# Prompt retention moved beside the gate projection; decode retention in column tiles; decode attention by itself

## What is computed

```python
# retention over the prompt, in 8 chunks of 128 tokens, 4 heads, key 256, value 512
def ret_chunk(S, q, k, v, log_gamma):
    qk = einsum('bihd,bjhd->bhij', q, k) * decay           # 128 x 128
    o = einsum('bhij,bjhe->bihe', qk, v)                   # inner part
    o = o + einsum('bihd,bhde->bihe', q * q_dec, S)        # part across chunks
    S_new = exp(C*log_gamma) * S + einsum('bjhd,bjhe->bhde', k * k_dec, v)
    return S_new, o
# the same function, once, for 8 samples of 8 tokens, each with its own state S (256 x 512 for each head)
# differential attention of 8 heads x 2 maps: the samples' new queries meet 512 cached keys and values
#   that lie in 4 pages of 128 rows, found through page_table
# merge: r = rms_plain(o) * silu(gr);  m = sigmoid(gate_a+b_a)*(a @ w_pa) + sigmoid(gate_b+b_b)*(r @ w_pb)
# h = h + m @ w_o;  h = h + swiglu(rms_norm(h));  y = rms_norm(h)
```

## Time and profile before

| | |
|---|---|
| runs, us | 3125.0, 3123.01, 3119.56 (median 3123.01) |
| profiled execution, us | 3118.55 |
| its span, first to last instruction, us | 3116.8 |
| PE, DVE, ACT, POOL busy | 95%, 33%, 20%, 30% |
| mean granted TensorE clock | 0.98 of full |
| the chain that ended last | PE 80%, issue 12%, DVE 4%, DMA 2% |
| gates beside decode retention, 965 to 1510 us | PE busy 540.05 of 545 us |
| between the stages, 1510 to 1526 us | PE busy 2.80 of 16 us |
| mixers, 1526 to 1868 us | PE busy 313.85 of 342 us |

### The profile page before, as it was taken

The page is one execution under the profiler, slowest core; times in us unless marked ns, Lnnn a source line. Parts: engine busy times, 40 slices in busy tenths (PEclk is TensorE's granted clock), DMA queues, the critical chain, the costliest instruction groups (busy, mean ns, idle before and its releaser), DMA issues.

```text
span 3116.8 us, 40394 instructions
## 1 busy us (share of the span) xinstructions
PE 2960.8 (95%) x15330; PEld 2439.5 (78%) x15330; DVE 1043.3 (33%) x1853; ACT 619.9 (20%) x1339; POOL 924.4 (30%) x782
## 2 busy tenths in 40 slices
PE   6999999999989999999797997999989999999998
PEld 4788887776766778777554557999779999998886
DVE  5430476566663121110133332242341111112323
ACT  3111111554542011111232331110120000001111
POOL 5334354022012223322200000443523343342521
PEclk9999999999999999999898998999989999999999
DMA  4332322332322433343566643443311221214311
GB/s 154 112 103 74 116 75 103 115 114 84 119 77 80 147 136 130 117 137 115 188 217 208 194 154 131 147 141 111 104 50 50 74 75 56 75 62 126 98 57 58
DMA packets 241445, 349.47 MB, mean 112 GB/s; under 512 B 26418, under 2 KB 138418, under 8 KB 241202
## 3 DMA queue, kind: packets, MB, share of 16 engines
q1 hardware_dynamic: 241330, 347.94, 33.5%
HBM read 249.91 MB, written 106.89 MB: 114 GB/s over the span
## 4 chain that ended last, share of the span: by engine, by line
PE 80%; issue 12%; DVE 4%; DMA 2%; POOL 1%; ACT 1%; SPq 0%; POOLq 0%; DVEq 0%; ACTq 0%
PE psum L438 38%; PE psum L414 25%; PE psum L940 5%; PE psum L979 2%; PE psum L1840 2%; PE psum L1003 2%; PE psum L1829 2%; PE psum L993 1%; POOL w_l L277 1%; PE psum L964 1%; POOL w_h L272 1%; DMA edge<-a_t 0%; PE psum L983 0%; DVE xt_l L2159 0%; DVE acc L2268 0%
## 5 line engine op out<-in xcount | busy, mean ns | idle before, releaser
L272 POOL TENSOR_TENSOR w_h<-stage,ones 128x512 fp32r<-128x512 f32 x372 | 416.9, 1151 | 1793.7 <-PE psum L438 950.9
L438 PE MATMUL psum<-xt_h,w_h 128*128 128x384 f32 (+1 forms) x2400 | 542.1, 334 | 23.7 <-DVE xt_l L2159 21.6
L438 PE MATMUL psum<-xt_h,w_l 128*128 128x384 f32 (+1 forms) x2400 | 529.5, 329 | 0.0
L438 PE MATMUL psum<-xt_l,w_h 128*128 128x384 f32 (+1 forms) x2400 | 529.1, 329 | 0.0
L277 POOL TENSOR_TENSOR w_l<-stage,w_h 128x512 fp32r<-128x512 f32 x372 | 491.6, 1352 | 7.4
L438 PEld LDWEIGHTS psum<-xt_h,w_h 128*128 128x128 f32 x2400 | 404.8, 189 | 101.2 <-issue 76.7
L414 PE MATMUL psum<-w_h,xt_h 128*128 128x512 f32 x1120 | 445.4, 398 | 17.0 <-ACTq L608 7.0
L414 PE MATMUL psum<-w_h,xt_l 128*128 128x512 f32 x1120 | 443.9, 396 | 0.0
L414 PE MATMUL psum<-w_l,xt_h 128*128 128x512 f32 x1120 | 443.7, 396 | 0.0
L438 PEld LDWEIGHTS psum<-xt_h,w_l 128*128 128x128 f32 x2400 | 408.5, 189 | 0.0
L438 PEld LDWEIGHTS psum<-xt_l,w_h 128*128 128x128 f32 x2400 | 408.0, 189 | 0.0
(11 more groups left out here) (212 smaller groups left out, 3227.5 us busy)
## 6 DMA issues: line engine op xcount, KB each, us to landing
stage<-in_w_in_dram SPq DMA_DIRECT2D x88, 512.0 KB, 5.9
proj<-edge SPq DMA_DIRECT2D x112, 256.0 KB, 2.0
stage<-in_w_gu_dram SPq DMA_DIRECT2D x44, 512.0 KB, 4.6
out_dram<-acc SPq DMA_DIRECT2D x40, 512.0 KB, 3.9
gates<-edge SPq DMA_DIRECT2D x32, 544.0 KB, 2.8
acc<-in_state_ret_dram SPq DMA_DIRECT2D x32, 512.0 KB, 5.2
k_page<-in_cache_k_dram SPq DMA_DIRECT2D x32, 512.0 KB, 5.8
v_page<-in_cache_v_dram SPq DMA_DIRECT2D x32, 512.0 KB, 6.4
```

Source lines behind the costliest of these rows:

```text
L272: last = nc.gpsimd.tensor_tensor(w_h[s][:, a:b, :], src, one.unsqueeze(1).to_broadcast([128, b - a, WN]), ALU.mult)
L438: ins = nc.tensor.matmul(psum[:, g(3 * j + c)[1], 0:width], w[s][:, k, m * 128:(m + 1) * 128], x[:, k, a:a + width], start=k == 0 and n == ...
```

## The change

Prompt retention leaves stage 2 and stands beside the gate projection, with decode retention, in one list that is written out without loops. Stage 2 keeps decode attention alone (and its functions are now `pe_decode`, `act_decode`, `dve_decode`, `sp_decode`).

- The unit of the gate projection is now one chunk of one row (24 matmuls in eight k steps), and the units use two PSUM banks in turn (`BG + q % 2`) in place of six. There are 768 k steps of three matmuls. A chunk of prompt retention has 21 of them (`BEAT`), after a lead of 96 (`LAG`, one head's rows).
- All 32 chunks run one after the other, in single buffers for q, k, the turned q and k, the state, the result and the gate.
- Decode retention takes four samples in one piece: eight matmuls of 16 output rows, in four column tiles of 32 partitions, in place of eight of 64 output rows (L1395, twice for each head). The state updates stay 64 matmuls (L1402).
- The reciprocal root of both is no longer POOL's power or ACT's square root: DVE takes it in ten small instructions on its own (`dve_root`).
- Decode attention has two buffers of key pages and two of value pages, and two pairs of banks for scores; the tail of a sample (weights, values) stands among the next sample's heads.
- POOL's retention loop is gone.

```diff
-                pe_feature_tile(pe, xt_h1, xt_l1, j, i * 4 + (2 * (W_FM + j) + 1),
-                                lambda c: (i * 24 + (G_FM + 12 * j + c), (G_FM + 12 * j + c) % RING),
-                                beside=lambda m, k: pe_n_piece(pe, i, 4 * j + m, k))
...
+        def gate_groups():
+            for q in range(3 * ROWS):
+                row, c = divmod(q, 3)
+                w, m, s, (a, width) = W_FM + row // 4, row % 4, row // 4 % 2, CHUNKS[c]
...
+                    pe.wait_ge(bank_free, RING + G_FM + q - 1)
+                for k in range(KD):
+                    sample_piece(row, 8 * c + k)
...
+                    for n, (wt, x) in enumerate(((w_h, xt_h1), (w_h, xt_l1), (w_l, xt_h1))):
+                        last = nc.tensor.matmul(psum[:, BG + q % 2, 0:width], wt[s][:, k, m * 128:(m + 1) * 128],
+                                                x[:, k, a:a + width], start=k == 0 and n == 0, stop=k == KD - 1 and n == 2)
...
+        for c in range(CHB):
+            update(c, 0)
+            inner(c)
+            gate(3)
+            if c:
+                rows_out(c - 1)
+            if c % NC:
+                across(c)
+            gate(4)
+            update(c, 1)
+            gate(3)
+            if c + 1 < CHB:
+                transposes(c + 1)
+            gate(4)
+            if c + 1 < CHB:
+                products(c + 1)
+            gate(7)
...
-            for b in range(KT):
-                last = nc.tensor.matmul(psum[0:TS, 7, :], q_own[:, b, m * TS:(m + 1) * TS], n_state[m % 4][:, b, :],
-                                        start=first and b == 0, stop=m == DB - 1 and b == KT - 1)
...
+                for b in range(KT):
+                    for j in range(4):
+                        last = nc.tensor.matmul(psum[32 * j:32 * j + 16, BA, :], q_own[:, b, g % 2 * 4 + j, :],
+                                                n_state[j][:, b, :], start=False, stop=m == 5 and b == KT - 1)
...
+    def dve_root(dve):
+        v, y, z = root_v, root_y, root_z
+        dstep.wait(dve)
+        dstep.done(nc.vector.tensor_scalar(root_seed, v.bitcast(I32), 1, None, ALU.logical_shift_right))
+        dstep.wait(dve)
+        dstep.done(nc.vector.tensor_scalar(y.bitcast(I32), root_seed, -1.0, float(0x5f3759df), ALU.mult, ALU.add))
+        dstep.wait(dve)
+        for c in (-3.0, -12.0, -768.0):
+            dstep.done(nc.vector.scalar_tensor_tensor(z, y, v, y, ALU.mult, ALU.mult))
+            dstep.wait(dve)
+            dstep.done(nc.vector.scalar_tensor_tensor(y, z, c, y, ALU.add, ALU.mult))
+            dstep.wait(dve)
+        dstep.done(nc.vector.tensor_scalar(y, y, -1.0 / 8192.0, None, ALU.mult))
+        dstep.wait(dve)
...
-    def pool_retention(pool):
-        with pool.Fori(0, RH * NC) as i:
-            pool.wait_ge(rvar_ready, i + 1)
-            nc.gpsimd.tensor_tensor(r_rstd[:, :], r_var[:, :], exponent[:, 0:1], ALU.pow).then_inc(rrstd_ready, 1)
...
+    k_page = [sb(f"k_page{s}", [128, NPG, D], F, st) for s in range(2)]
+    v_page = [sb(f"v_page{s}", [128, NPG, D], F, st) for s in range(2)]
...
+        for s in range(DB + 1):
+            for h in range(DH + 1):
+                if s < DB and h < DH:
+                    page(s, h)
+                if s < DB and h:
+                    scores(s, h - 1)
+                if s and h == 2:
+                    weights(s - 1)
+                if s and h == 4:
+                    outputs(s - 1)
+                if s and h == 6:
+                    outputs_t(s - 1)
```

More of the change, by code:

```diff
@@ L517, in sp_project @@
             sp.wait_ge(stored[s], 16 * (1 + N_TM * NT // 3))
[L520 to L547, removed]
+        sp_gates(sp)
     VR_I = 5
     G_TM = 0
-    G_FM = banks_before(W_FM)
     def pe_project(pe):
@@ L610, in act_project @@
         act.wait_ge(roped, 8 * NT + 6)
[L612 to L634, removed]
+        act_gates(act)
     dstep = Count(dve_step)
@@ L713, in dve_project @@
         dve.wait_ge(a_ready, 2 * DH)
[L714 to L735, removed]
+        dve_gates(dve)
     NQ = TP // 128
@@ new lines, in hybrid_layer, with __init__, to, chunk_kg @@
+    n_ready = sem("n_ready")
+    class Beside:
+        def __init__(self, steps):
+            self.steps = steps
+            self.at = next(steps, None)
+        def to(self, kg):
+            while self.at is not None and self.at < kg:
+                self.at = next(self.steps, None)
+    def chunk_kg(c):
+        return LAG + BEAT * c
+    UPDATES = {(1, 10): (0, 0), (1, 15): (0, 1), (1, 20): (1, 0), (2, 1): (1, 1),
+               (2, 6): (2, 0), (2, 11): (2, 1), (2, 16): (3, 0), (2, 21): (3, 1)}
@@ L1362, in store_state, with load_pages @@
[L1362 to L1371 removed]
+        def load_pages(numbers, j, x, cache, loaded):
+            for p in range(NPG):
+                sp.dma_start(x[j][:, p, :], cache[bass.ds(numbers[p], 1), :, :].rearrange("o p d -> (o p) d")).then_inc(
+                    loaded[j], 16)
@@ L1372, in sp_mixers @@
+        for s in range(DB):
+            numbers = [sp.value_load(pages[0:1, s * NPG + p:s * NPG + p + 1], min_val=0, max_val=N_PHYS - 1)
+                       for p in range(NPG)]
+            if s >= 2:
+                sp.wait_ge(s_full, s - 1)
+            load_pages(numbers, s % 2, *keys)
+            if s >= 2:
+                sp.wait_ge(s_out_full, s - 1)
+            load_pages(numbers, s % 2, *vals)
         sp.wait_ge(s_norm, 5)
@@ new lines, in page, with scores @@
+        def page(s, h):
+            if h == 0:
+                pe.wait_ge(kp_loaded[s % 2], 64 * (s // 2 + 1))
+            pe.wait_ge(page_ready, max(DH * s + h - 1, 0))
+            for p in range(NPG):
+                last = nc.tensor.transpose(psum[:, BP + h % 2, p * 128:(p + 1) * 128],
+                                           k_page[s % 2][:, p, h * 128:(h + 1) * 128], ident[:, :])
+            last.then_inc(page_full, 1)
+        def scores(s, h):
+            if h == 0:
+                pe.wait_ge(wide_ready, s + 1)
+                pe.wait_ge(s_exp, max(s - 1, 0))
+            pe.wait_ge(page_ready, DH * s + h + 1)
+            q, banks = q_wide[:, h * 128:(h + 1) * 128], score_banks(s)
+            nc.tensor.matmul(banks[:, 0, :], q, page_t[h % 2][:, :], start=h == 0, stop=h == DH - 1)
+            last = nc.tensor.matmul(banks[:, 1, 0:TS], q, k_new_t[:, h, :], start=h == 0, stop=h == DH - 1)
+            if h == DH - 1:
+                last.then_inc(s_full, 1)
@@ L1681, in dve_mixers @@
+        widen(0)
+        for s in range(DB):
+            maximum(s)
+            if s + 1 < DB:
+                widen(s + 1)
+            combination(s)
+            outputs(s)
         dve.wait_ge(s_out_read, DB)
```

1126 lines of the change are left out of this document (588 added, 538 removed).

## The result

| | before | after |
|---|---|---|
| median of the runs, us | 3122.91 (3119.56 to 3125.0) | 3046.33 (3043.34 to 3047.79) |
| profiled execution, us | 3118.55 | 3047.79 |
| its span, us | 3116.8 | 3046.0 |
| gate stage: first gate matmul to the end of PE's last piece | 967.22 to 1510.87: 543.7 | 968.09 to 1637.67: 669.6 |
| stage 2, up to DVE's `o_square` | 359.7 | 161.1 |

The gate stage's end is the start of its last four transposes and what they take: 1510.41 + 0.46 before, 1637.23 + 0.44 after. The ratio is 0.9755, 95% interval 0.9738 to 0.9771: 76.6 us less. The forecast was 3096, in a range of 3077 to 3122. The sign was right and two thirds of the gain were not foreseen.

The account below looks back on a forecast made before the run. PE, busy 95% of the span, was taken as the bound. Gate stage 712 plus 12 of root waits and stage 2 at 155 gave -25 us, about 3096; range 3077 to 3122, the forecast's own 3082 to 3112.

Parts of the forecast that it names:

- the price of a break: Gate stage: fp32 pieces between fp32r passes cost PE 0.34 to 0.39 us extra, 45 us for prompt retention.
- The roots: Gate stage: DVE root chains slowed by POOL's splits make PE wait 12 us in total, bounds 0 and 69.
- rival A: Gate stage: the delays hide, with no waiting for roots and most of the unexplained 7 us gone; 3080 us, chance 0.20.
- Rival B: Gate stage: roots behind POOL's splits set the pace, seven splits costing PE 9.8 us each; 3153 us, chance 0.08.
- 380.6 for the gates: Gate stage: 2304 fp32r matmuls of the gate projection take PE 380.6 us, before and after.
- the updates at 1.25: Gate stage: 64 decode-state updates cost PE 1.25 us each, 80.0 us in all, before and after.
- column tiles side by side: Gate stage: decode sample pieces run four column tiles at a time, taking 16.5 us against 65.9.
- Rival C: Decode attention: page loads set the pace, 146 us in place of 125; 3117 us in all, chance 0.10.
- Stage 2: Decode attention alone: start 19, clock restart 2, heads and tails 125, last tail 8.6; 155 us in all.
- delayed page copies: Decode attention: at each sample's start the softmax delays two page copies, 0.6 us each time, 4.2 in all.
- The last tail: End of decode attention: the last sample's weights, values and seven short ACT and DVE steps stand uncovered, 8.6 us.
- The start: Start of decode attention: from the gate stage's last PE work to the first key page, 19 us against 22.9.

Follow-up runs that it names:

- e1: Changed kernel with the decode-state updates contracting over 128 rows, the lower 64 zeros: 3022.6 us, 23.7 less than the changed kernel.
- e2: Kernel before the change with decode updates padded to 128 rows and sample matmuls writing 128 output rows: 3087.68 us, 36.1 less than that kernel.
- e7: Changed kernel with the prompt-state updates cut to 64 of their 128 rows: 3068.1 us, 21.8 more than the changed kernel.
- e4: Changed kernel with every root chain on DVE run twice: 3090.72 us, 44 more; with every chain run four times: 3233.94 us, 188 more.
- e3: Changed kernel with most matmuls of the decode-sample pieces put on one column tile instead of four: 3076.02 us, 29.7 more.
- e5: Changed kernel with one key-page and one value-page buffer in decode attention instead of two of each: 3119.41 us, 73 more.

## Why the prediction was wrong

**The failed step: the price of a break.** The gate stage's sum was 380.6 + 218.4 + 106.3 + 7 = 712. In 218.4 stood 45 us of breaks for prompt retention. The runs show a break to be the tile's shape: 0.34 to 0.39 us for each piece that is not 128 by 128 (e1: 23.7 / 64; e2: 36.1 / 92; e7: 21.8 / 64), none for fp32 between fp32r, where L1459 takes the 0.86 of its work. Every piece that I had priced in the earlier trace rows was 64 rows or 64 output columns; prompt retention's are 128 by 128. I gave the bound 0 for this term but stayed at the measured price, which was measured on something else. The row says so itself, `64*128` and `128*64` against `128*128`. With 173.3 in place of 218.4 the sum is 380.6 + 173.3 + 106.3 = 660.2; the stage took 669.6, of which 2.6 are waits for DVE, and 7 are left over, as they were before. Part of those are waits for loads, 2.3 us after (L1376) and 3.0 before (L1812), which the sums did not have.

The range failed at the same term. It named 0 as the bound of the breaks and then began at 30; and 30 with roots at 0 is already 3096 - 15 - 12 = 3069, not 3082. With both bounds at 0 the forecast's own low end is 3039, and the measured 3046 lies above it.

The forecast had the right rule in hand. The Trainium skill, "TensorEngine Tiling (Array Packing)", Key Properties, says that a change of tiling mode drains TensorE. The three runs agree, with 0.34 to 0.39 us for both ends of a piece. I applied it to the eight column-tile pieces alone. Applied to the 64-row tiles of the earlier trace rows as well, it would have explained the break there, and left none for prompt retention.

**The roots**: right in mechanism, mis-sized. Of the 12 us 2.6 came (rival A had none, and comes nearest of the rivals with 3080). The slow instructions are only those with two operands in SBUF, six of ten, and in the chain above five of these six; the sixth, at 1040.18, took its usual 0.16. Of the kernel after, the whole-span rows of L1602 and, for one with a single tensor operand, L1606:

```profile
L1602 DVE SCALAR_TENSOR_TENSOR o_newton<-o_rstd,o_var x108: 219/220/1328, 1039.0 to 1630.1; 128x1 f32<-128x1 f32 x108
```

```profile
L1606 DVE TENSOR_SCALAR o_rstd<-o_rstd x36: 153/154/155, 1045.3 to 1630.5; 128x1 f32<-128x1 f32 x36
```

The Trainium skill, "SBUF — State Buffer", Who interferes with whom, says that a VectorE instruction with two SBUF inputs contends with a GpSimd instruction that reads SBUF, and one with a single SBUF input outside the two-port modes does not. The two rows agree, up to 1328 ns against at most 155; the forecast named the rule and still charged the whole chain. Rival B was wrong as it stood and near: e4 shows that one more chain costs 44 us, so delays of this kind do reach PE once the chain is longer, and the kernel's own chain stays below that.

**Right**: 380.6 for the gates; the updates at 1.25; column tiles side by side (e3), 65.9 to 16.5, the largest gain. Rival C is out: after the first page no wait names a page, and two buffers were needed for that (e5). **Stage 2**: 161.1 for 155. A sample's period is 16.68 (1675.05 to 1691.73) against 16.2, which makes 3.4 of the 6 us. In place of the 0.6 that the forecast put down to delayed page copies stands a wait for DVE's wide queries (L1942), 0.5 idle and 0.8 from start to start; the rest is 0.05 to 0.09 at several changes from one kind of piece to the next. The last tail is open for 11.2 us in place of 8.6. The start, 18.1 for 19, was right.

The account: 903.4 us of both stages before, 830.7 after, is -72.7. Column tiles give 49. Prompt retention costs 173.3 in either place, by the prices of single pieces, so moving it is free on PE. What PE stood or was held in stage 2 beyond its own work (359.7 - 173.3 - 94.1 - 26.7 - 3.8 = 61.8 before, 161.1 - 94.1 - 26.7 - 3.8 = 36.5 after) gives 25. Beside the gates some 2 us more are lost than before. The forecast took these same two gains and set 57 us of breaks and roots against them, which were 2.6.

The best version run is e1, 3022.6 us: the change, and the decode updates padded to 128 rows.

## What to carry to other kernels

Before a measured surcharge is carried over to other instructions, compare every field of the rows it came from, the tile's shape among them; if all of them share a property that the new ones lack, the surcharge may belong to that. Where small pieces stand between passes of a full 128 by 128 tile, padding theirs with zeros to 128 rows and columns costs no columns and saves the break, here 24 us for three memsets; it does not pay where the smaller tiles run side by side, as the column tiles do. A queue that is busy for 40% can be at its threshold all the same: lengthen the suspected chain and shorten it, and the two runs say on which side the kernel stands.

## What was not expected of the hardware

- Half the rows and half the output columns break alike, or nearly: 0.39 and 0.34 from start to start in the earlier trace rows, 0.39 a piece over both kinds in e2, 0.37 for rows alone in e1. No run changed the columns alone.
- A wait of TensorE came with more time than itself: 29 us more of waits in e4 with a gate stage 44 us longer, 55 us in e5 with a stage 2 longer by 71, at granted clocks of 0.975 and 0.970 over the span against 0.981. That the clock makes the difference is not shown by a run of its own.
- Under a GpSimd split of 1.04 to 1.29 us an instruction, a VectorE instruction of 0.22 us with two SBUF operands took up to 1.33, however small it is (128x1), while the one with a single operand right behind a slow one took its usual 0.15 (1045.28), with the next split instruction running since 1045.19.
